# Cached attention in a hybrid decoder step: absorbed queries made earlier, upward weights kept on chip, page table loaded earlier, pages loaded without a staging ring

## What is computed

```python
def mla_keys_values(ckv, kpe, w_kv_up, g_kn):
    kv = (ckv @ w_kv_up).reshape(ckv.shape[:-1] + (N_HEADS, QK_NOPE + V_HEAD))
    k_nope, v = kv[..., :QK_NOPE], kv[..., QK_NOPE:]
    k_pe = jnp.broadcast_to(kpe[..., None, :], k_nope.shape[:-1] + (QK_ROPE,))
    return rmsnorm(jnp.concatenate([k_nope, k_pe], axis=-1), g_kn), v

def one_sequence(a):                     # for each of the 8 decode sequences
    pt, q1, c1, r1 = a
    c_all = jnp.concatenate([ckv_pool[pt].reshape(past, KV_LORA), c1], axis=0)
    r_all = jnp.concatenate([kpe_pool[pt].reshape(past, QK_ROPE), r1], axis=0)
    k, v = mla_keys_values(c_all, r_all, *kv_w)
    return causal_attend(q1, k, v, q_pos, k_pos)
```

## Time and profile before

| | |
|---|---|
| median of 3 runs | 3112.68 us (3109.79 to 3114.93) |
| profiled execution: device time | 3104.88 us |
| profiled execution: span, first to last instruction | 3103.0 us |
| PE busy | 2942.7 us (95% of the span) |
| DVE, ACT, POOL busy | 1919.0, 970.5, 459.9 us |
| projections, prompt attention, cached attention | to about 228, 425 and 1001 us of the span |

### The profile page before, as it was taken

One profiled execution on the slowest core, in us unless ns is written; L12 is line 12 of the kernel. 1 busy time (PEld: TensorE's weight loads), 2 busy tenths in 40 slices (PEclk: granted clock), 3 DMA queues, 4 the chain that ended last, 5 costly groups with the idle time before them and its releaser, 6 DMA issues. The chain is left out here.

```text
span 3103.0 us, 54816 instructions
## 1 busy us (share of the span) xinstructions
PE 2942.7 (95%) x19232; PEld 2756.9 (89%) x19232; DVE 1919.0 (62%) x3783; ACT 970.5 (31%) x1739; POOL 459.9 (15%) x652
## 2 busy tenths in 40 slices
PE   7979879999998899999999988999989999999998
PEld 4646669998897899999999988989989999999998
DVE  2446658777776466556666666882346566666665
ACT  3434335555554332222222223222222222222221
POOL 1003312211220000000000008660000000000000
PEclk9988989999998899999999999999999999999999
DMA  3110012222221111111111105344112111111111
GB/s 103 34 19 4 35 54 79 73 73 73 71 72 51 32 55 42 48 41 47 47 47 41 48 25 155 86 105 125 43 49 62 42 41 54 41 47 41 54 34 68
DMA packets 262505, 175.44 MB, mean 57 GB/s; under 512 B 77961, under 2 KB 247642, under 8 KB 262058
## 3 DMA queue, kind: packets, MB, share of 16 engines
q1 hardware_dynamic: 262314, 173.03, 19.3%
HBM read 150.54 MB, written 22.29 MB: 56 GB/s over the span
## 5 line engine op out<-in xcount | busy, mean ns | idle before, releaser
L1615 PE MATMUL f_up<-h_hi,f_wu_hi 128*128 128x352 f32 x2112 | 460.2, 326 | 16.8 <-DVE h_lo L2133 15.1
L1615 PE MATMUL f_up<-h_hi,f_wu_lo 128*128 128x352 f32 x2112 | 457.3, 324 | 0.0
L1615 PE MATMUL f_up<-h_lo,f_wu_hi 128*128 128x352 f32 x2112 | 457.0, 325 | 0.0
L1615 PEld LDWEIGHTS f_up<-h_hi,f_wu_hi 128*128 128x128 f32 x2112 | 361.8, 190 | 18.0 <-issue 15.7
L1615 PEld LDWEIGHTS f_up<-h_hi,f_wu_lo 128*128 128x128 f32 x2112 | 364.6, 189 | 0.0
L1615 PEld LDWEIGHTS f_up<-h_lo,f_wu_hi 128*128 128x128 f32 x2112 | 360.9, 189 | 0.0
L2046 ACT ACTIVATE f_conv<-f_u_row,f_taps 128x1056 f32<-128x1056 f32 x88 | 111.8, 1271 | 754.3 <-DVE f_u_row L2163 754.3
L2232 DVE TENSOR_TENSOR resid<-resid,f_down 128x352 f32<-128x352 f32 x528 | 271.6, 518 | 110.1 <-PE f_down L1992 107.1
L1992 PE MATMUL f_down<-f_a_hi,f_wd_hi 128*128 (+1 forms) x960 | 318.1, 331 | 6.2 <-DVE resid L2232 5.8
L1992 PE MATMUL f_down<-f_a_hi,f_wd_lo 128*128 (+1 forms) x960 | 310.3, 323 | 0.0
L1992 PE MATMUL f_down<-f_a_lo,f_wd_hi 128*128 (+1 forms) x960 | 310.0, 323 | 0.0
(11 more groups left out here) (424 smaller groups left out, 5796.9 us busy)
## 6 DMA issues: line engine op xcount, KB each, us to landing
f_wu<-ffn_w_up SPq DMA_DIRECT2D x86, 512.0 KB, 3.9
ca_ring<-cache_ckv SPq DMA_DIRECT2D x256, 128.0 KB, 2.0
raw<-ffn_w_down SPq DMA_DIRECT2D x44, 512.0 KB, 4.4
raw<-ssm_w_out SPq DMA_DIRECT2D x16, 512.0 KB, 3.8
s_spill<-resid SPq DMA_DIRECT2D x8, 528.0 KB, 10.5
s_u<-sm_ut SPq DMA_DIRECT2D x8, 528.0 KB, 2.6
resid<-s_spill SPq DMA_DIRECT2D x8, 528.0 KB, 7.2
pj_xb<-x_prompt SPq DMA_DIRECT2D x8, 512.0 KB, 3.6
```

The costliest lines, as they stand in the source:

```text
L1615: mm = nc.tensor.matmul(out(c), w, x(c), start=(first and n == 0), stop=(last and n == 2))
```

## The change

In the projections, `w_in` comes in four quarters ahead of five of the six small loads, DVE waits for its own gain alone and scales `w_in` first, and POOL copies the first block before it scales `w_q`. In the last step PE makes the queries and keys of the last block ahead of turning the heads of the one before, then turns the key part of the upward weights; ACT copies that to `raw` and `inv`. `w_kv` stays on chip. The page table is loaded in the prompt's stage, into memory that the result uses later. PE makes the absorbed queries in the first head of the prompt's stage and DVE keeps them. In the cached stage SP starts with the pages, ACT issues the spreading DMAs, pages land straight in `cache` (rows of 257 numbers, 1028 bytes a page and partition), POOL copies nothing, `values` stands after page 20 of a step, and the output weights are loaded at the end of the stage. Its core:

```diff
@@ project, sync
+            sp.dma_start(g_x[:, :], ...).then_inc(g_x_in, 16)
+            for part in range(4):
+                k = slice(2 * part, 2 * part + 2)
+                sp.dma_start(w_in[:, k, :], w_src[:, k, :]).then_inc(w_in_in[part], 16)
...
-            for half in range(2):
-                k = slice(half * KT // 2, (half + 1) * KT // 2)
-                sp.dma_start(w_in[:, k, :], w_src[:, k, :]).then_inc(w_in_in[half], 16)
+            load_x(1)
@@ project, gpsimd
+            step(0)
+            pool.wait_ge(wts_in, 16 * 5)
             pool.wait_ge(wq_in, 16)
@@ project, tensor
+            def turn_key_weights():
+                heads = w_kv[:, :, :].rearrange("p k (h d) -> p k h d", h=H)
+                pe.wait_ge(pj_kept, NB)
+                for k, bank in enumerate((pj, pq)):
+                    if k == 1:
+                        pe.wait_ge(qk_kept, NB)
+                    for h in range(H):
+                        mm = nc.tensor.transpose(bank[0:NOPE, h // 4, (h % 4) * P:(h % 4 + 1) * P], heads[:, k, h, 0:NOPE], ident[:, :])
+                    mm.then_inc(wk_turned, 1)
...
+                if ends:
+                    queries(i - 1)
+                    keys_values(i - 1)
                 if in_range(i, 2, NB):
...
+                if ends:
+                    turn_key_weights()
@@ project, scalar (after head_squares of the last block)
+            def keep_key_weights():
+                act.wait_ge(x_stored, NB)
+                for k, (dst, bank) in enumerate(zip(keep["wkT"], (pj, pq))):
+                    act.wait_ge(wk_turned, k + 1)
+                    nc.scalar.activation(dst[0:NOPE, 0:H * P].rearrange("p (a n) -> p a n", a=2), bank[0:NOPE, :, :], ACT.Copy).then_inc(wk_kept, 1)
@@ project, vector
-            dve.wait_ge(wts_in, 16 * 6)
+            dve.wait_ge(g_x_in, 16)
...
+            scale_rows()
             block_scale(0)
             block_inverse(0)
-            scale_rows()
+            dve.wait_ge(wts_in, 16 * 5)
@@ attend_prompt, sync
+            sp.dma_start(keep["table"][:, :], io["page_table"]).then_inc(tab_in, 16)
             prep.on_sync(sp, io, prep_dram)
+            sp.wait_ge(tab_in, 16)
@@ attend_prompt, tensor
+            def cached_queries(k):
+                for h in range(H):
+                    mm = nc.tensor.matmul(out[:, 1, (k * H + h) * TS:(k * H + h + 1) * TS], keep["wkT"][k][0:NOPE, h * P:(h + 1) * P],
+                                          qT_s[0:NOPE, h, :], start=True, stop=True)
+                mm.then_inc(qc_done, 1)
...
                     score(h, half, i)
+                    if first and i < KK:
+                        cached_queries(i)
@@ attend_prompt, vector
                     row_top(h, i)
+                    if first and i == KK - 1:
+                        keep_cached_queries()
@@ attend_cache, sync
-            sp.dma_start(table[:, :], io["page_table"]).then_inc(tab_in, 16)
-            sp.dma_start(w_kv[:, :, :, :], ...).then_inc(w_in, 16)
-            sp.wait_ge(rope_put, 1)
-            for y in range(GP):
-                sp.dma_start(q_rep[y * ROPE:(y + 1) * ROPE, :, :], q_rope[NOPE:QKH, :, :]).then_inc(rope_rep, 16)
-            sp.wait_ge(tab_in, 16)
...
-                    sp.wait_ge(stored, (g - RG + 1) * GP)
+                    if p == 0:
+                        sp.wait_ge(pages_free, (g - RG + 1) * GP)
...
-                sp.dma_start(ring[:, p % (GP * RG), :], io["cache_ckv"][0, phys]).then_inc(page_in[at], 16)
+                sp.dma_start(cache[:, b % 2, p, 0:KVL], io["cache_ckv"][0, phys]).then_inc(page_in[at], 16)
...
+            sp.dma_start(w_out[:, :, :], io["attn_w_out"][0].rearrange("(k p) n -> p k n", p=P)).then_inc(w_out_in, 16)
+            sp.wait_ge(w_out_in, 16)
@@ attend_cache, gpsimd
-                if p == 0 and (not isinstance(b, int) or b >= 2):
-                    pool.wait_ge(pv_done, b - 1)
...
-                nc.gpsimd.tensor_copy(cache[:, b % 2, p, 0:KVL], ring[:, p % (GP * RG), :]).then_inc(stored, 1)
@@ attend_cache, tensor
-            for h in range(H):
-                for k in range(KK):
-                    mm = nc.tensor.transpose(kn[0:NOPE, k, h // 4, (h % 4) * P:(h % 4 + 1) * P], w_kv[:, k, h, 0:NOPE], ident[:, :])
...
-            for h in range(H):
-                for k in range(KK):
-                    mm = nc.tensor.matmul(misc[:, (k * H + h) * TS:(k * H + h + 1) * TS], wkT[:, h, k * P:(k + 1) * P], qT_s[0:NOPE, h, :], start=True, stop=True)
...
+                    mm.then_inc(pages_free, NPAGE)
...
+            pe.sem_inc(pages_free, NPAGE - (RG - 1) * GP)
             turn_page(0, 0)
+            pe.wait_ge(ready, 1)
             turn_kpe(0, 0)
+            pe.wait_ge(ready, 1 + GP)
             rope_scores(0, 0)
...
-                stream(b, page, {3: sum_mass, 5: turn_mean, 8: turn_top, 11: spread_top})
-                values(b)
+                stream(b, page, {3: sum_mass, 5: turn_mean, 8: turn_top, 11: spread_top, 20: values})
@@ attend_cache, scalar
-            act.wait_ge(w_in, 16)
+            act.wait_ge(rope_put, 1)
+            for y in range(GP):
+                act.dma_start(q_rep[y * ROPE:(y + 1) * ROPE, :, :], q_rope[NOPE:QKH, :, :]).then_inc(rope_rep, 16)
+            nc.scalar.activation(qc_hi[:, :, :, :], qc, ACT.Copy).then_inc(qc_kept, 1)
...
@@ attend_cache, vector: gather, s_new and the rope queries now stand before the low parts of the weights
@@ add_attention, sync
-            sp.dma_start(w[:, :, :], io["attn_w_out"][0].rearrange("(k p) n -> p k n", p=P)).then_inc(w_in, 16)
```

More of the change, by code:

```diff
@@ L124, in project @@
         wts_in = sem("wts_in")
-        w_in_in = [sem("w_in_in0"), sem("w_in_in1")]
+        w_in_in = [sem(f"w_in_in{i}") for i in range(4)]
+        g_x_in = sem("g_x_in")
         wq_in = sem("wq_in")
@@ L191, in step @@
             def step(i):
-                if in_range(i, -1, NB):
+                if in_range(i, -1, NB) and not (isinstance(i, int) and i == 0):
                     load_x(i + 1)
@@ L300, in step @@
                     turn_heads(i - 2, 0, q_turned)
-                if in_range(i, 1, NB):
+                if in_range(i, 1, NB) and not ends:
                     queries(i - 1)
@@ L1672, in add_attention @@
         NTURN = len(turn)
-        w_in = sem("w_in")
         first_in = sem("first_in")
```

134 lines of the change are left out of this document (65 added, 69 removed).

## The result

The kernel after takes 3090.11 us (median of six runs, 3083.85 to 3097.19) against 3110.09 for the kernel before beside it: a ratio of 0.9944, interval 0.9927 to 0.9961. Nine more runs gave 3093.46 against 3109.15 (twenty runs, 3093.63 to 3114.29): 0.9952, interval 0.9934 to 0.9970. So the gain is about 15 us, and single runs of one kernel spread over 20. The profiled execution took 3085.36 us.

A forecast was written before the change was run, and what follows sets the result against it. The prediction took PE to bound the cached loop, and chains of transfers and copies the setups. Its terms summed to -9.4 us, which set on the median 3112.68 gave 3103.3, with a range of 3093 to 3112.

The forecast's parts named there:

- the first product: Start of the projections: PE's first product was to begin near 10.4 us instead of 14.66, a term of -4.3.
- the first transposes: Prompt's start: first transposes some 4.6 later against the stage's start, since the absorbed queries stand before them, +4.6.
- the absent row near 1.2: Cached loop: no DVE scaling of scores near 1.2 us once POOL's copies go, a term of -1.0.
- the boundaries didn't eat the gain: Rival, chance 0.08: PE waits at six sequence boundaries for most of 4.09, costing 22, total 3125.
- the prompt did pay: Rival, chance 0.20: earlier clock rise makes the prompt's queries free and the start gains 5.9; -15.6, total 3097.
- the setup's next wait: Rival, chance 0.17: cached setup's rope queries and low parts delay first page to 439, slow pages cost 2; total 3109.
- the start moved: Against a rival, chance 0.05: the start does not move, as something else paces w_in's transfer; -5.1, total 3107.6.
- Output weights: Output stage: early loading removes ACT's wait of 1.91 for them, -1.9, bounds 0 and -3.
- End of the cached loop's boundaries: Cached loop: +1.0 for half a page at a colder clock, +2.4 for six boundaries at 0.4, -1.0 for POOL's copies.
- End of the projections: Projections' last step: queries fill PE's gap, 16 transposes and two ACT copies are new; +0.3, bounds -1.9 and +1.9.
- Setup of the cached stage: Before the first cached page: first page turn moves from 447.08 to 435.0, -12.0, bounds -8 and -13.
- the tail: End of the cached stage: tail begins 1.5 after the last page while 4.26 of values stand in the stream, +1.5.

The follow-up runs named there:

- late load: The kernel after with the output weights loaded at the start of the output stage, as before: 3095.10 us, ratio 0.9967 to the kernel before.

## Why the prediction was right and wrong

**Right**: the direction and the mechanism. The gain is waiting in the setups; the loop paid for DVE's lost breath at one boundary only, POOL's copies in step were worth nothing to PE, and the queries in the prompt were bare. Of the marks that I named, the first product (10.1), the first transposes (4.2 later, 6.6 where the clock was lower), the absent row near 1.2 and ACT's missing wait came. Two missed by a little: the first page came about 1 sooner after the stage's start than the 9.6 that I gave, and PE's wait at the start of the fifth sequence was 1.6, not under 0.5 (0.3 at the others). None of the rivals happened: the boundaries didn't eat the gain, the prompt did pay, the setup's next wait was the pages and not the low parts, and the start moved.

**Wrong**: the size, by some 5 of 14 us, and the range. The largest miss is the step that took ACT's wait for the output weights as the whole of their price. Four terms of the sum were each sized too dearly.

1. *Output weights*, -1.9 forecast, -3.3 measured. The step read ACT's visible wait as the whole price. The late load shows that the wait is only what the transposes leave of the landing (1.91 in the first profile before, where they ran at the lower clock; 3.67 and 3.41 in the two others without the early load and 3.18 here, at the upper), and that PE's clock fell in the longer wait. So the one profile that I read showed the smallest wait of the four. With the early load the transposes ran at the upper level in nine of ten profiles. My bound of -3 was short as well.
2. *End of the cached loop's boundaries*: 1.0 (clock) + 2.4 (six boundaries) - 1.0 (copies) = +2.4 forecast, +1.1 measured. The step "0.4 at each of six boundaries" failed: one jump of the loop costs about 1.6 more, in a second wait of PE and, in six of eight profiles, a longer stay at the lower clock; the other boundaries cost nothing, and the copies had nothing to give back. Half a page (1.0) for a colder clock came in some executions only: with the lower level 4.6 to 5.1 us into the pages (5.0 to 5.9 before) the first sequence took 61.2 to 61.5, with 7.1 to 7.4 it took 62.5.
3. *End of the projections*, +0.3 forecast, -0.9 measured. The queries were to fill PE's gap of 7.76; they wait 5.82 of it for ACT. The transposes and copies were charged, at the lower clock's durations, though both lie where PE and ACT wait for DVE. Undoing the order shows that it is worth 1.0 and that the rest is free.
4. *Setup of the cached stage*, -12.0 forecast, -13.1 measured. The 8.0 from SP's first issue to the landed group came from a stretch in which one issue took 1.09 in place of 0.33; without it 7.25. SP's first issue also came 1.2 after the stage's start (423.2) and not 1.6. That the chain of rope queries and low parts is level with the pages was right: its last part for the weights ended 0.8 behind the first page turn.

Only the tail erred the other way (+2.4 for +1.5), by less than it varies itself. The sum failed because I took a cautious value at each place; errors of one sign add up.

The place on the scale failed as well. I set -9.4 on 3112.68, the median of three runs; twenty gave 3109.15, which is 3.5 of the miss. Against the nine later runs (3093.46) the miss is 9.8: 4.7 from the terms, 3.5 from the place, and 1.6 that I can't assign; the first six runs came out another 3.4 lower. And the range of 19 us was built from bounds of the terms alone: code that the change doesn't touch moves by 14 us from one execution to the next, so the median of a few runs is itself uncertain by several us.

## What to carry to other kernels

Cut several profiles of both kernels at the same instructions before explaining a difference: here one pair showed 2.4 us in code that was the same. A wait behind a late transfer is worth what the transfer is late, not the rest that is seen after other work, and an engine without work has its clock to lose too. Work added where an engine already waits for another was free here, or nearly so; look for such a gap (here the 7.5 us ahead of the first page) before placing it where an engine is busy. And compare two stretches at the same granted clock: the prompt's cost of the queries came out as 4.2 that way, while single profiles gave anything from 1.3 to 7.2.

## What the runs showed of the hardware that was not expected

- The clock's level in identical code: 2974 matmuls of the state-space stage at 0.97 or 0.94, 421.8 to 436.6 us. In that stage the records of the granted clock add up to between 22.6 and 56.6 us at the lower level, with seven to nine stops of PE in it. The Trainium skill (TensorE: Matmul & The Clock Gate, What you observe) gives a scatter of half a microsecond either way from run to run for one rise of the clock; in the whole of this stage these runs show a spread of fifteen.
- One jump back in a loop over sequences cost PE 1.9 to 2.6 us. With the values in mid-sequence 0.6 to 1.6 of waiting for DVE or ACT followed, and then 3.4 to 6.8 us at the lower level of the clock; written out, the period fell by about 5.5. What in the jump takes so long no view shows.
- Single DMA issues stretched from 0.33 to between 1.09 and 1.53 (in the setups of three kernels), and four issues on ACT's queue from 2.53 to 2.99, 3.45 and 3.48. It moved the first page by 1 us. With what they collide isn't shown.
